# First token mixer on un-normalised columns of x, root mean square applied at the banks, short convolution in two halves

## Reference

```python
def rmsnorm(x, g):
    y = x * lax.rsqrt(jnp.mean(x * x, axis=-1, keepdims=True) + EPS)
    return y * g

def token_mixer(hn, ...):            # hn = rmsnorm(x, ln1_g[l])
    p = hn @ w_in
    xc, gb_c, gc_c, q, k, v, g_out, a_low, gate_a, gate_b = split(p)
    y_a = gb_c * short_conv(gc_c * xc, conv_w)        # 3 taps, causal, per channel
    log_a = log_sigmoid(a_low @ w_a2 + b_a) / TAU     # decay
    o = gla(q, k, v, log_a)                           # gated linear attention, chunks of 64
    y_b = rmsnorm(o, gla_norm_g) * silu(g_out)
    merged = sigmoid(gate_a) * (y_a @ w_branch[0]) + sigmoid(gate_b) * (y_b @ w_branch[1])
    return merged @ w_out
```

## Time and profile before

| what | us |
|---|---|
| median of three runs (1408.29 to 1408.36) | 1408.29 |
| the profiled execution | 1408.48 |
| its span | 1406.7 |
| TensorE busy in it | 1394.4 |
| DVE, ACT, GpSimd busy | 440.0, 301.6, 135.3 |

### The profile page before, as it was taken

One profiled execution on the slowest core, in us unless ns is written; L12 is line 12 of the kernel. 1 busy time (PEld: TensorE's weight loads), 2 busy tenths in 40 slices (PEclk: granted clock), 3 DMA queues, 4 the chain that ended last, 5 costly groups with the idle time before them and its releaser, 6 DMA issues.

```text
span 1406.7 us, 34725 instructions
## 1 busy us (share of the span) xinstructions
PE 1394.4 (99%) x16039; PEld 870.3 (62%) x16039; DVE 440.0 (31%) x724; ACT 301.6 (21%) x425; POOL 135.3 (10%) x167
## 2 busy tenths in 40 slices
PE   9999999999999999999999999999999999999997
PEld 7999999999999983353353354354354344344344
DVE  6775775555777563110110110110110110110121
ACT  6554454444646430000000000000000000000000
POOL 2650000000463000000000000000000000000000
PEclk9999999999999999999999999999999999999999
DMA  9755566666565549999999999999999999999995
GB/s 329 253 180 181 180 195 195 207 204 190 173 201 195 192 160 358 417 418 419 417 419 419 416 419 411 412 420 410 412 421 410 413 420 408 414 421 408 421 420 202
DMA packets 132014, 462.73 MB, mean 329 GB/s; under 512 B 8531, under 2 KB 66545, under 8 KB 117538
## 3 DMA queue, kind: packets, MB, share of 16 engines
q1 hardware_dynamic: 126290, 449.87, 82.4%
q0 software_dynamic: 2448, 7.94, 1.5%
q10 hardware_dynamic: 3136, 2.75, 0.6%
HBM read 455.68 MB, written 4.86 MB: 327 GB/s over the span
## 4 chain that ended last, share of the span: by engine, by line
PE 96%; DVE 2%; issue 0%; DMA 0%; ACT 0%; POOL 0%; SPq 0%; POOLq 0%; DVEq 0%
PE banks L1602 95%; PE banks L1765 1%; DMA x<-in_x_dram 0%; DVE w_lo L819 0%; PE banks L1637 0%; DVE mem L1078 0%; POOL ors L1555 0%; DVE mem L855 0%; DVE mem L1115 0%; ACT mem L670 0%; PE banks L1867 0%; PE banks L1735 0%; PE banks L1798 0%; ACT mem L577 0%; DVE mem L1108 0%
## 5 line engine op out<-in xcount | busy, mean ns | idle before, releaser
L1602 PE MATMUL banks<-mem 128*32 128x448 f32 (+2 forms) x11712 | 878.4, 462 | 0.1
L1602 PEld LDWEIGHTS banks<-mem 128*32 128x32 f32 (+1 forms) x11712 | 381.5, 110 | 494.6 <-issue 377.1
L819 DVE TENSOR_TENSOR w_lo<-mem,w_hi 128x1024 fp32r<-128x1024 f32 x178 | 224.1, 1279 | 112.5 <-ACT w_hi L553 111.3
L1438 DVE TENSOR_TENSOR mem<-mem,banks 128x448 f32<-128x448 f32 x48 | 26.9, 616 | 716.2 <-PE banks L1602 716.2
L1602 PE MATMUL banks<-xt_hi,w_hi 128*128 128x256 f32 x832 | 230.1, 277 | 0.0
L1602 PE MATMUL banks<-xt_lo,w_hi 128*128 128x256 f32 x832 | 228.8, 275 | 0.0
L1602 PE MATMUL banks<-xt_hi,w_lo 128*128 128x256 f32 x832 | 228.8, 275 | 0.0
L553 ACT CAST w_hi<-mem 128x1024 fp32r<-128x1024 f32 x178 | 184.3, 1048 | 159.1 <-PE banks L1602 156.9
L1602 PEld LDWEIGHTS banks<-xt_hi,w_hi 128*128 128x128 f32 x832 | 159.6, 192 | 1.1 <-issue 0.3
L1602 PEld LDWEIGHTS banks<-xt_lo,w_hi 128*128 128x128 f32 x832 | 159.7, 192 | 0.3
L1602 PEld LDWEIGHTS banks<-xt_hi,w_lo 128*128 128x128 f32 x832 | 159.7, 192 | 0.0
(11 more groups left out here) (228 smaller groups left out, 703.3 us busy)
## 6 DMA issues: line engine op xcount, KB each, us to landing
mem<-in_eg_dram SPq DMA_DIRECT2D x128, 896.0 KB, 13.1
mem<-in_eu_dram SPq DMA_DIRECT2D x128, 896.0 KB, 12.9
mem<-in_ed_dram SPq DMA_DIRECT2D x112, 1024.0 KB, 15.2
mem<-in_w_in_dram SPq DMA_DIRECT2D x38, 1024.0 KB, 5.5
mem<-in_fg_dram SPq DMA_DIRECT2D x11, 1024.0 KB, 5.3
mem<-in_fu_dram SPq DMA_DIRECT2D x11, 1024.0 KB, 5.3
mem<-in_fd_dram SPq DMA_DIRECT2D x11, 1024.0 KB, 4.9
mem<-in_w_br_dram SPq DMA_DIRECT2D x8, 1024.0 KB, 5.5
```

The costliest lines, as they stand in the source:

```text
L819: nc.vector.tensor_tensor(w_lo[:, q % H, :], src, w_hi[:, q % H, :].bitcast(F32), ALU.subtract).then_inc(lo_done, 1)
L1438: nc.vector.tensor_tensor(h, h, by_pair(bank[3 + g]), ALU.mult).then_inc(ehf_done, 1)
L1602: return nc.tensor.matmul(out, lhs, rhs, start=first, stop=last, skip_group_check=True)
```

## The change

First mixer. The host passes x turned as well (`xt`: 128 partitions, 8 columns of gain, then 8 blocks of 256 tokens). SyncE asks for it in three parts among the value weights (1, 1, 1, 1, 2 and 2 row blocks of 128), and for x itself behind chunk 2. ACT and DVE split gain times x (no root) into x0_hi and x0_lo, and the value weights in halves of a piece. Values, low rank and all units up to gb1 use these. The root mean square is made from x later, spread over all partitions by a product (`spread_root`, between the halves of the q unit), and multiplied in where a unit is read from its bank: values by ACT, low rank, q, k and xc by DVE (q, k and xc were read by ACT). xc gets the root squared, which stands for gc's as well; gb's root is multiplied in behind the taps. For go and the gates, which take xt_hi and xt_lo as before, DVE scales the columns in place and DVE and ACT split them. Transposes, the gain's spread and the scaling by tokens fall away; eleven warm-ups stand in a row at the start. GpSimd asks for low-rank weights, taps, bias and w_a2 behind the landing of value rows 4 and 5, and for constants, GLA gain and router's weights behind the root.

Both mixers. The taps of two blocks of channels stand right behind their own gate product.

```diff
+        x0_hi, x0_lo = (area[:, n * 2048:(n + 1) * 2048].rearrange("p (k t) -> p k t", k=KT) for n in (0, 1))
+        value_landed = value_in[0:3] + [raw_in[0], value_in[3], value_in[3], raw_in[1], raw_in[1]]
@@ SyncE
+            columns(0, 0, KT + 2 * SEQ)
+            value_rows(0, 1, value_in[0])
+            value_rows(1, 1, value_in[1])
+            columns(1, KT + 2 * SEQ, KT + 4 * SEQ)
+            value_rows(2, 1, value_in[2])
+            value_rows(3, 1, raw_in[0])
+            columns(2, KT + 4 * SEQ, KT + 8 * SEQ)
+            value_rows(4, 2, value_in[3])
+            value_rows(6, 2, raw_in[1])
...
                     load(c + n, unit_rows(l, n))
+                    if l == 0 and n == 2:
+                        for t in range(TB):
+                            sp.dma_start(x[:, t, :], x_d[0, t * P:(t + 1) * P, :]).then_inc(x_in[t], 16)
@@ ACT, l == 0
+                    for kk in range(KT):
+                        weighed_high(kk)
+                        half_split(kk)
...
                     act.wait_ge(al_in, 16)
                     nc.scalar.copy(al_both[:, :, :, 0:RANK], al_raw).then_inc(al_hi, 1)
-                    until(H + 2)
+                    until(H)
+                    norm_squares(0, (0, 2))
+                    until(H + 4)
...
+                if l == 0:
+                    after(2)
+                    normed_high(0)
+                    after(4)
+                    normed_high(1)
+                    after(5)
@@ DVE, l == 0
+                    for kk in range(KT):
+                        weighed_low(kk)
+                        half_low(kk)
...
                     until(H)
+                    own_half(0)
+                    own_half(1)
+                    dve.wait_ge(rs_full, 1)
+                    step(nc.vector.tensor_copy(rs_row, bank[7][:, 0:SEQ]))
...
+                    nc.vector.tensor_tensor(own_al, al_turned, rs_turned[0:2 * RANK, :, :], ALU.mult).then_inc(al_done, 1)
+                    step(nc.vector.tensor_tensor(rs_squared, rs_row, rs_row, ALU.mult))
+                    until(H + 2)
...
+                if l == 0:
+                    until(H + 3)
+                    src = full(l, "q")
+                    for h in range(HP):
+                        ins = nc.vector.scalar_tensor_tensor(out=qT[:, h, :].rearrange("p (b a) -> p b a", b=2),
...
+                    until(H + 4)
                 dve.wait_ge(log_done, l + 1)
...
                 ins.then_inc(b_done, 1)
                 if l == 0:
+                    after(1)
+                    per_token(kT, full(l, "k"), rs_row).then_inc(k_done, 1)
+                    after(2)
+                    normed(0)
+                    after(3)
+                    for n in range(2):
+                        after(4 + n)
+                        per_token(cv[:, 2 * n:2 * n + 2, :], full(l, f"xc{n}"), rs_squared).then_inc(xc_done, 1)
+                        if n == 0:
+                            normed(1)
+                        normed_low(n)
...
                     dve.wait_ge(gc_done, 2 * l + n + 1)
-                for j in range(TAPS):
-                    for b in range(CB):
...
+                    own_blocks = range(2 * n, 2 * n + 2)
+                    for j in range(TAPS):
+                        for b in own_blocks:
...
+                        step(ins)
+                    if l == 0:
+                        own_cv = cv[:, 2 * n:2 * n + 2, :]
+                        step(nc.vector.tensor_tensor(own_cv, own_cv, rs_row.unsqueeze(1).to_broadcast([P, 2, SEQ]), ALU.mult))
@@ GpSimd
-                root(2 * l)
                 if l == 0:
+                    pool.wait_ge(value_in[3], 16)
                     nc.gpsimd.dma_start(al_raw.rearrange("p l k r -> p (l k r)"), w_al_d[:, :]).then_inc(al_in, 16)
...
+                    root(0)
                     nc.gpsimd.dma_start(const[:, K_BASE:K_END], const_d[:, K_BASE:K_END]).then_inc(params_in, 16)
@@ TensorE
+            keep_warm(11)
...
+                    for kk in range(KT):
+                        first_values(kk)
+                    low_rank(claim(l, "alow"), l, (x0_hi, x0_lo))
...
+                            pe.wait_ge(rs_done, t + 1)
+                            ins = mm(bank[7][:, t * P:(t + 1) * P], rs[:, t:t + 1].to_broadcast([P, P]), ident, True, True)
+                        ins.then_inc(rs_full, 1)
+
+                    channels(claim(l, "q"), base + 4, of=(x0_hi, x0_lo), between=spread_root)
...
+                    if l == 0 and n < 10:
+                        channels(claim(l, WIN[n][0]), base + 2 * n, of=(x0_hi, x0_lo))
+                        return
...
+                if l == 0:
+                    pe.wait_ge(xn_l, 2)
                 outs = [claim(l, f"go{t}") for t in range(TB)]
```

More of the change, by code:

```diff
@@ L431, in unit_rows, with columns, value_rows @@
                 return rows(w_in_d[l], 0, KT, col, 256)
[L433 to L437, removed]
+            def columns(n, first, end):
+                sp.dma_start(g_xt[:, first:end], xt_d[:, first:end]).then_inc(xt_in[n], 16)
+            def value_rows(k0, nk, landed):
+                dst = raw(k0 // 4, k0 % 4 * 512, 512 * nk).rearrange("p (k n) -> p k n", k=nk)
+                sp.dma_start(dst, rows(w_in_d[0], k0, nk, C_V, 512)).then_inc(landed, 16)
+            columns(0, 0, KT + 2 * SEQ)
[7 more added lines that the diff above has]
+            value_rows(6, 2, raw_in[1])
             for l in range(DEPTH):
@@ L632, in _ @@
                 nc.scalar.activation(eb[:, :, :], bb[:, :, :], ACT.Exp, scale=1.0 / TAU).then_inc(eb_done, 1)
[L633 to L642, removed]
+                if l == 0:
[4 more added lines that the diff above has]
+                    after(5)
+                else:
+                    after(2)
+                    src = full(l, "q")
+                    nc.scalar.mul(halves(qT[:, :, :]), unturned(src[:, :], HP), DK ** -0.5).then_inc(q_done, 1)
+                    after(3)
+                    src = full(l, "k")
+                    nc.scalar.copy(halves(kT[:, :, :]), unturned(src[:, :], HP)).then_inc(k_done, 1)
+                    for n in range(2):
+                        after(4 + n)
+                        src = full(l, f"xc{n}")
+                        nc.scalar.copy(halves(cv[:, 2 * n:2 * n + 2, :]), unturned(src[:, :], 2)).then_inc(xc_done, 1)
                 for h in range(HP):
@@ new lines, in normed, with normed_low @@
+                    def normed(half):
+                        for kk in range(4 * half, 4 * half + 4):
+                            ins = nc.vector.scalar_tensor_tensor(out=x_cols[:, kk, :], in0=x_cols[:, kk, :],
+                                                                 scalar=g_cols[:, kk:kk + 1], in1=rs_row[:, :],
+                                                                 op0=ALU.mult, op1=ALU.mult)
+                        ins.then_inc(xn_made, 1)
+                    def normed_low(half):
+                        kk = 4 * half
+                        dve.wait_ge(xn_h, half + 1)
+                        nc.vector.tensor_tensor(xt_lo[:, kk:kk + 4, :], x_cols[:, kk:kk + 4, :],
+                                                xt_hi[:, kk:kk + 4, :].bitcast(F32), ALU.subtract).then_inc(xn_l, 1)
@@ L1512, in _ @@
                     nc.gpsimd.dma_start(wr_raw[:, :], w_r_d[:, :]).then_inc(params_in, 16)
+                else:
+                    root(2 * l)
                 for h in range(HP):
@@ L1639, in transposes, with channels @@
                 ins.then_inc(turned, 1)
-            def channels(out, q0, blocks=2, counts=(None, None), ready=None):
+            def channels(out, q0, blocks=2, counts=(None, None), ready=None, of=(xt_hi, xt_lo), between=None):
                 for half in range(2):
+                    if half and between is not None:
+                        between()
                     w = piece(q0 + half, counts[half])
@@ L1689, in low_rank @@
                 for kk in range(KT):
-                    for xt in (xt_hi, xt_lo):
+                    for xt in of:
                         ins = mm(out[0:2 * RANK, 0:SEQ], al_both[:, l, kk, :], turns(xt[:, kk, :]),
-                                 kk == 0 and xt is xt_hi, kk == KT - 1 and xt is xt_lo)
+                                 kk == 0 and xt is of[0], kk == KT - 1 and xt is of[1])
                 ins.then_inc(al_full, 1)
             pe.wait_ge(init_done, 1)
-            keep_warm(3)
-            pe.wait_ge(init_done, 2)
-            pe.wait_ge(gain_in, 16)
-            for h in range(2):
-                ins = nc.tensor.matmul(bank[6 + h][:, :], one_row, gain[0:1, 512 * h:512 * h + 512], start=True, stop=True)
-                ins.then_inc(gain_spread, 1)
-            keep_warm(2, bank[3])
-            pe.wait_ge(ident_made, 1)
+            keep_warm(11)
             for l in range(DEPTH):
```

214 lines of the change are left out of this document (119 added, 95 removed).

## The result

Changed kernel: **1412.89 us**, median of 8 runs (1411.82 to 1413.84); before 1408.29 (8 runs, 1408.01 to 1408.67). The ratio is 1.0031, 95% interval 1.0022 to 1.0040: about 4.6 us slower, past the 0.2% named in the prediction, and 0.1 us past the upper end of its range. The profiled execution of the changed kernel took 1412.89 us, its span is 1411.1, 4.4 more than before.

What follows compares the result with a forecast made beforehand. TensorE, busy 99% of the span, was taken as the bound, with DVE deciding whether an earlier front survives. The 1408.3 us before plus 1.3 us of later TensorE work gave 1409.6 us, range 1405.2 to 1412.8.

Steps and rivals of the forecast that it cites:

- Step 1: Front, up to the product with w_a2: ends at 27.7 us instead of 31.0, so 3.3 us earlier.
- Step 2: Scan of the decays: ends at 34.5 us, not 30.6; scores(0) still finds its operands.
- Step 3: DVE from scan to second gate product: done at 69.7 us, so the go units start 1.1 us later.
- TensorE would be there at 67.3 and waits 2.4: Ahead of the go units: TensorE arrives at 67.3 us and waits 2.4 us for the second gate product.
- rival (d): First values: TensorE's clock stays at its lower level, costing all but hidden waits about 0.5 us; chance 0.06.
- (b): Ahead of the scan: constants land late, at 35 us, everything 1.8 us later, 1411.4 us in all; chance 0.17.
- (c): DVE beside GpSimd: the contention price applies everywhere, +2.6 us, 1410.9 us in all; chance 0.17.
- Step 4: Behind the gate products: piece 22 loses 0.4 us, y's low part ends at 86.4, TensorE carries on 1.3 us late.
- rival (a): The front's gain survives with cheaper taps and columns: transposes at 83.0 us, 3.1 us less, 1405.2 us; chance 0.20.
- Step 5: Second mixer: conv in halves leaves the gate product 5.7 us ahead of the go units; zero effect.
- (e): The prediction's own case, 1409.6 us in all; chance 0.40.
- the signs named: Whole trace: among others, a TensorE wait over 1 us for the root and DVE over 90% busy from 34 to 75.

Runs made afterwards that it cites:

- experiment 6: Changed kernel with ACT's first exponential of the decays moved ahead of the second normalised high part: 1414.96 us, ratio 1.0047.
- Experiment 1: Changed kernel with 18 products of zeros put where TensorE waits ahead of the go units: 1410.28 us, ratio 1.0014.
- experiment 4: Changed kernel with DVE's order in the first mixer changed, both gate products ahead of any conv: 1411.61 us, ratio 1.0023.
- 10: The version of experiment 8 without its early exponential, so ACT's order and both gate products first: 1406.85 us, ratio 0.9990.
- Experiment 3: The kernel before with only the conv in halves, in both mixers: 1408.36 us, ratio 1.0001.
- experiment 8: Changed kernel with three reorderings together (ACT's order, first exponential early, both gate products first): 1405.31 us, ratio 0.9978.
- experiment 11: The version of experiment 8 with three warm-ups instead of eleven: 1405.88 us, ratio 0.9982.
- 5: Changed kernel with ACT's order alone changed in the first mixer, pieces ahead of the scan's exponential and the normalised high parts: 1407.03 us, ratio 0.9992.
- 2: Changed kernel with the first mixer's conv in one block behind both gate products, as before: 1411.81 us, ratio 1.0024.
- 9: Changed kernel run once more without an edit: 1412.25 us, ratio 1.0027.
- 7: Changed kernel with the reorderings of experiment 4 and experiment 6 together: 1408.05 us, ratio 0.9998.

## Why the prediction was right or wrong

**Step 1, right.** 3.3 us predicted, 3.4 measured; values from 6.57 (6.0 to 6.6), low rank from 17.94 (17.4), the w_a2 product's end 27.63 (27.7). Its parts were less good, and the start was right by luck: the eleven warm-ups were over at 5.21 and held nothing, and TensorE waited 1.36 us for DVE's first low part of the weights, because the first columns reached ACT at 4.56, not 3.35. The wait for the root was 0.25 us, not 1.5, and low rank started 0.5 late.

**Step 2, right.** The scan ended at 34.1 (34.5). GpSimd's first exponents took 7.8 us (34.19 to 41.96), not 12.9; that harmed nothing, because ACT was the one late at the exponential (54.49).

**Step 3, right for DVE, wrong for TensorE.** The second gate product ended at 69.74, as forecast (69.7). The sum came out with errors that cancel: the twelve pieces took 16.6 us instead of 15.0, the half conv with the root 5.0 instead of 4.3, the waits for ACT 4.2 instead of 5.1, the scan was 0.4 early, and where one row follows another they overlap by about 0.1 us, which the sum left out (0.8 in all). The columns cost 3.95 us (2.29 and 1.66 for four each, so 0.57 and 0.42 apiece), nearly as taken. The Trainium skill, GPSIMD Engine Reference, the specification table, names contention between GpSimd and DVE instructions with two SBUF inputs. The prediction's price for it, 0.69, wasn't reached in the changed kernel, though 0.57 beside GpSimd against 0.42 beside an idle one shows some of it; in experiment 6 it was passed, with 0.90 apiece. (Eight at 0.69 are also 1.6 us above the 3.9 taken, not 1.3.) The step that failed is **"TensorE would be there at 67.3 and waits 2.4"**. From 27.63, seven units of 5.37 give 65.2, and only 0.7 went to waits on the way, where I had put 2.0. So TensorE was there at 65.89 and waited 4.1, while the go units started at 70.02, nearly as forecast (69.8). An arrival that is padded with losses is no cautious figure when a wait is its difference to another's.

**The term that was missing** is the granted clock behind that wait. I had asked about the clock for the first values only (rival (d)) and let the go units keep their 10.4 us; they took 13.4. Experiment 1 puts a price on it, 2.6 us, by taking it away alone. In the traces the go units start 1.4 late and last 3.0 longer, which is the span's 4.4; the sum had 1.1 for the start, 0.4 for piece 22, and nothing for the clock. At the slower pace piece 22 was in time, and TensorE didn't wait for it. So the measured time lies at the edge of the range by luck: the upper end, 1412.8, was added up from rivals (b) and (c), and neither came.

**Step 4, mechanism right, no longer on the path.** y's low part was done at 86.66 (86.4), but TensorE came to the transposes only at 89.95, not 87.0. (87.0 is 1.4 behind the 85.56 of before, where the sum carries on 1.3.) Experiments 4 and 10 show that this is the second limit once the first is gone, as rival (a) had it, with waits of 3.4 and 1.0 us.

**Step 5, right.** In the second mixer the gate product ended at 412.2, 4.5 us ahead of the go units (5.7 forecast), and nothing waits. Experiment 3 confirms zero for the halves in both mixers.

**Rivals.** (a) did not happen, though its result did in experiment 8 (1405.31 against its 1405.2), by reordering and not by cheaper instructions; its 83.0 at the transposes is 2.6 ahead of 85.56, not the 3.1 that it counts. (b) is out: the scan stood behind DVE's own work, with no wait for the constants. (c) is true of single instructions and did not decide in the changed kernel, DVE's total was as forecast; in experiment 6 it did, where GpSimd ran beside other DVE work. (d) is out in the changed kernel, and experiment 11 shows what the eleven warm-ups had prevented: about the 0.6 us between two medians, itself not clear of noise, for which the rival gave 0.5. The chance of slower, 0.26, was made up of (b), a third of (c) and some of (e) and (d). The late start of the go units is (e)'s own; the clock that falls behind the wait is in none of them. Of the signs named, the wait for the root was under 1 us, and DVE was busy for 89% of the time from 34 to 75, just short of the 90% named. The cause of the 4.6 us is shown by 1, 4, 5 and 8: DVE is done about 4 us behind TensorE's arrival, through its waits for ACT (5) and through the conv half ahead of the gate product (4), and the clock falls behind that wait (1). 4 alone was not enough, because the next limit stands right behind.

## What to carry to other kernels

When a change brings a saturated engine earlier to a point where another engine's result is needed, compute both arrivals, without padding either, and look at the next such point as well. Price a wait of several microseconds on TensorE at more than its length: here one of 4.1 us cost another 2.6. When helpers are reordered, ask what then runs beside what: experiment 6 moved GpSimd's work out of the conv and into the column scaling, and lost. And before giving up such a change, look at the order of the helpers' queues: an order tuned for the old start gave back more than the front had won, and three small moves in it turned 4.6 us lost into 3.2 us gained.

## What the runs showed of the hardware that was not expected

- **Waits and the clock.** Waits of TensorE of 3.4 us (experiment 4), 3.8 (2), 4.0 (6) and 4.1 (changed kernel, 9) were each followed by a stretch at the lower clock; waits of 1.0 (10), 1.2 (5) and 1.3 us (6, 7) by none. Where it begins is open. Nor is the stretch always the same. In the changed kernel, 9 and 6 the clock fell while TensorE still waited and stayed at 0.50 for 6.8 us; in 2 and 4 it fell about 1 us after TensorE had started again and stayed there for 3.4 us (1-us windows of 2: 0.94 from 75 to 76, 0.50 up to 79, 0.86 up to 80). In 11 a start with three warm-ups and 3.9 us of waiting gave 0.43 us per product, in the changed kernel eleven and 1.36 us of waiting gave 0.22.
- **GpSimd and DVE.** Exponents in the changed kernel beside an idle DVE, beside a piece and beside the column scalings, and a later product of 128x512 (GpSimd's timeline, same columns):

```profile
35.65 0.39 POOL L1632 TENSOR_TENSOR mem<-mem 128x128 f32<-128x128 f32 x1
36.01 1.46 POOL L1633 TENSOR_TENSOR mem<-mem 128x128 f32<-128x128 f32 x1
...
38.77 0.63 POOL L1633 TENSOR_TENSOR mem<-mem 128x128 f32<-128x128 f32 x1
...
56.95 2.27 POOL L1647 TENSOR_TENSOR mem<-mem 128x512 f32<-128x512 f32 x1
```

0.39 us where DVE idles, 1.46 beside pieces of 128x1024, 0.63 beside 128x256. So a DVE that waits speeds GpSimd up, and the 12.9 us of before could not be carried over. It goes the other way too. The fourteen pieces between 34 and 76 us, by duration (minimum, median, maximum in ns):

```profile
L868 DVE TENSOR_TENSOR w_lo<-mem,w_hi x14: 1217/1266/2308, 36.0 to 75.1; 128x1024 fp32r<-128x1024 f32 x14
```

The longest, 2.3 us (58.00 to 60.31), ran beside the end of GpSimd's 128x512 shown above (to 59.22) and a 128x128 that took 1.44. Such a piece is nearly twice as long as one alone (1.22); the 1.37 taken from before is a mean over eight pieces beside GpSimd's exponents, and no price for other neighbours.
